# The shared expert's down product made while combining, two experts' first weights loaded while routing

## What is computed

```python
def swiglu(t, wg, wu, wd):
    return (jax.nn.silu(t @ wg) * (t @ wu)) @ wd

def moe_ffn(t, router_w, router_bias, w_gate, w_up, w_down, sh_gate, sh_up, sh_down):
    scores = jax.nn.sigmoid((t @ router_w).astype(jnp.float32))
    _, idx = lax.top_k(scores + router_bias.astype(jnp.float32), TOP_K)
    wts = ... / jnp.sum(wts, axis=-1, keepdims=True) * ROUTED_SCALE
    ...
    routed = jnp.zeros((n_tok, d), jnp.float32).at[buf_tok].add(y)   # y: swiglu of each expert's rows * weight
    shared = swiglu(t, sh_gate, sh_up, sh_down).astype(jnp.float32)
    return (routed + shared).astype(t.dtype)

x = x + gf_x * moe_ffn(h_x, *moe_args).reshape(x.shape)
return rms_norm(x, final_norm_g)
```

## Time and profile before

| what | value |
|---|---|
| median of three runs | 2757.75 us |
| the profiled execution's own time | 2765.79 us |
| its span in the trace | 2764.1 us |
| shared_and_route, first to last VectorE work | 1534.3 to 1650.1 us |
| of it, from the placed rows to the next phase | 1621.5 to 1653.8 us |
| experts | 1653.8 to 2641.4 us |
| combine | 2641.5 to 2764.1 us |
| TensorE busy over the whole span | 2502.3 us (91%) |
| DMA over the whole span | 408.11 MB, mean 148 GB/s |

### The profile page before, as it was taken

How to read it: one execution, slowest core, us unless ns; L and a number is a source line. 1 busy time by engine, 2 the same in 40 slices (tenths; PEclk the granted TensorE clock), 3 DMA queues, 4 the chain that set the end, 5 groups by cost and what they waited for, 6 DMA issues and landing times. The chain is left out here.

```text
span 2764.1 us, 72353 instructions
## 1 busy us (share of the span) xinstructions
PE 2502.3 (91%) x27195; PEld 1374.4 (50%) x27196; DVE 1542.4 (56%) x2685; ACT 973.6 (35%) x1707; POOL 840.7 (30%) x654
## 2 busy tenths in 40 slices
PE   5999899889799699899889788899999999999956
PEld 2448358735599545799644343333333333333322
DVE  3106365843578603566634676566666666666538
ACT  2613115512222112333111104455555555555411
POOL 1000000000255100111000004566666666666565
PEclk9999998989999899999889998999999999999978
DMA  6001402120000110000122127999998899672187
GB/s 254 9 0 47 140 16 92 49 63 16 1 4 4 28 48 1 3 5 4 64 100 92 58 79 315 347 353 350 367 353 317 322 343 346 260 273 83 69 320 311
DMA packets 109099, 408.11 MB, mean 148 GB/s; under 512 B 21001, under 2 KB 37083, under 8 KB 83932
## 3 DMA queue, kind: packets, MB, share of 16 engines
q1 hardware_dynamic: 76636, 287.71, 28.5%
q0 software_dynamic: 20736, 75.51, 7.0%
q10 hardware_dynamic: 11520, 41.95, 3.7%
HBM read 346.40 MB, written 58.72 MB: 147 GB/s over the span
## 5 line engine op out<-in xcount | busy, mean ns | idle before, releaser
L3271 PE MATMUL bank<-arena 128*32 x1280 | 570.0, 599 | 9.0 <-ACT arena L3338 5.9
L3273 PE MATMUL bank<-arena 128*32 128x512 f32 x3840 | 571.1, 599 | 0.0
L3232 POOL COPY arena<-arena 128x2048 f32 x240 | 450.4, 1910 | 331.3 <-PE bank L3305 314.3
L3271 PEld LDWEIGHTS bank<-arena 128*32 128x32 f32 x1280 | 135.1, 110 | 358.9 <-issue 349.9
L3302 PE MATMUL bank<-arena 128*32 x640 | 290.6, 597 | 5.5 <-POOL arena L3232 5.5
L3305 PE MATMUL bank<-arena 128*32 128x512 f32 x1920 | 291.7, 597 | 0.0
L3426 DVE COPY arena<-arena 128x2048 f32 x80 | 138.4, 1731 | 205.5 <-PE bank L3273 181.4
L3363 ACT COPY arena<-arena 128x2048 f32 x80 | 152.0, 1900 | 200.4 <-PE bank L3273 133.5
L3222 POOL DMA_INDIRECT arena<-normed_rows,arena x80 | 163.8, 2048 | 149.5 <-DVE arena L3410 137.5
L1262 PE MATMUL bank<-arena 64*64 64x64 f32 x4480 | 165.3, 220 | 13.6 <-DVE arena L1334 5.4
L3302 PEld LDWEIGHTS bank<-arena 128*32 128x32 f32 x640 | 70.5, 110 | 198.7 <-issue 198.2
(11 more groups left out here) (555 smaller groups left out, 4652.3 us busy)
## 6 DMA issues: line engine op xcount, KB each, us to landing
arena<-in_exp_w_gate_dram SPq DMA_DIRECT2D x64, 1024.0 KB
arena<-in_exp_w_up_dram SPq DMA_DIRECT2D x64, 1024.0 KB
arena<-in_exp_w_down_dram SPq DMA_DIRECT2D x64, 1024.0 KB
expert_rows<-arena ACTq DMA_DIRECT2D x80, 512.0 KB
arena<-in_w_mod_dram SPq DMA_DIRECT2D x32, 512.0 KB, 10.9
arena<-in_x_dram SPq DMA_DIRECT2D x16, 512.0 KB, 8.5
arena<-in_w_mod_dram SPq DMA_DIRECT2D x8, 1024.0 KB, 17.6
arena<-in_w_in_dram SPq DMA_DIRECT2D x12, 384.0 KB
```

Of the source, the lines that this page charges most:

```text
L3232: last = nc.gpsimd.tensor_copy(down_copy(u), down_of(slots[u]))
L3271: nc.tensor.matmul(out(SUB - 1), XTT[:, b.q, c, rows(SUB - 1)], W[:, :, c], start=first, stop=end)
L3273: last = nc.tensor.matmul(out(u), XTT[:, b.q, c, rows(u)], WC[:, u, :, c], start=first, stop=end)
```

## The change

The shared down product leaves shared_and_route. Its hidden rows `HID` are stored to a new DRAM tensor `hid_dram` (two stores of 512 KB), and `X1` is stored right at the start of the phase, as it is. In combine TensorE makes the product of a tile at the head of the tile's group in the same two banks, before the five gathered rows are added (four products of 128x512 per tile). The gate multiply and the add into `X1` that combine has anyway then cover both.

What combine reads (`X1` 4 MB, `HID` and the shared down weights 1 MB each) is loaded in the experts' phase, once the last experts' slots are free, into the slots of experts 59 to 62. `ACC` and `OUT` of combine lie in the slot of expert 63.

Gate and up of experts 0 and 1 are loaded in shared_and_route. For that the ring lies at the top of SBUF, shifted by one slot, so the slot table gets one more add.

In the last block the three copies of the downs are made by VectorE, ScalarE and GpSimd, one each.

```diff
@@ shared_and_route: the loads and stores of SP
             sp.dma_start(WU, kc(wu[0])).then_inc(gu_in, 16)
-            sp.dma_start(WD, wd[0].rearrange("(p c) n -> p c n", c=2)).then_inc(d_in, 16)
+            for e in range(BEFORE):                                  # BEFORE = 2
+                gate_up_to(sp, WGU, exp_wg, exp_wu, bass.ds(e, 1), e, first)
             for t in range(XT):
-                sp.wait_ge(base, 2 * t + 2)
                 sp.dma_start(base_dram[t * P:(t + 1) * P, :], X1[:, t]).then_inc(st, 16)
+            for f in range(2):
+                sp.wait_ge(hid, 2 * f + 2)
+                sp.dma_start(hid_dram[:, f * SEQ:(f + 1) * SEQ], HID[:, f]).then_inc(hid_st, 16)
             sp.wait_ge(st, 16 * XT)
+            sp.wait_ge(hid_st, 32)
+            sp.wait_ge(first, 32 * BEFORE)
@@ TensorE
-            pe.wait_ge(d_in, 16)
-            pe.wait_ge(hid, 4)
-            for n in range(2 * XT):
...
-                for f in range(2):
-                    last = nc.tensor.matmul(ps[1 + n % 4][:, :], HID[:, f, t * P:(t + 1) * P],
-                                            WD[:, f, half * 512:(half + 1) * 512], start=(f == 0), stop=(f == 1))
-                last.then_inc(dn, 1)
@@ VectorE
-            nc.vector.tensor_reduce(bx[:, 0], nb_le[:, :, 0:NE - 1], AX.X, ALU.add).then_inc(bex_t, 1)
+            chain(nc.vector.tensor_reduce(bx[:, 0], nb_le[:, :, 0:NE - 1], AX.X, ALU.add))
+            TS(bx[:, 0], bx[:, 0], float(SLOT0), None, ALU.add).then_inc(bex_t, 1)
...
-            for n in range(2 * XT):
...
-                TT(T[:, n % 2], ps[1 + n % 4][:, :], k.gate[1][:, c], ALU.mult).then_inc(out, 1)
-                dve.wait_ge(out, n + 1)
-                TT(X1[:, n // 2, c], X1[:, n // 2, c], T[:, n % 2], ALU.add).then_inc(base, 1)
@@ experts: SP
             for e in range(RING):
-                gate_up(bass.ds(e, 1), e)
+                if e < BEFORE:
+                    sp.sem_inc(loaded[e], 32)
+                else:
+                    gate_up(bass.ds(e, 1), e)
                 down(bass.ds(e, 1), e)
...
+            for n, e in enumerate((NE - 5, NE - 4, NE - 3)):
+                copied, read = released(e)
+                if n == 2:
+                    hold(sp, hi_d, copied)
+                    hold(sp, hi_a, copied)
+                    hold(sp, up, read)
+                    sp.dma_start(HS, hid_dram).then_inc(late_in, 16)
+                    sp.dma_start(WS..., sh_down...).then_inc(late_in, 16)
+                hold(sp, dcopy, copied)
+                hold(sp, dn, read)
+                for t in (2 * n, 2 * n + 1):
+                    sp.dma_start(tiles[t], base_dram[t * P:(t + 1) * P, :]).then_inc(late_in, 16)
...                                                # tiles 6 and 7 after expert NE - 2
+            sp.wait_ge(late_in, 16 * (XT + 2))
@@ experts: the last block (GpSimd copies only piece SUB - 2 there)
+            pe.wait_ge(last_d, 1)
+            pe.wait_ge(last_a, 1)
             widen(Turn.at(NBLK - 1))
@@ ScalarE, after the last fold
+            act.wait_ge(dn, LAST_B + 1)
+            nc.scalar.copy(down_copy(1), down_of(slot)).then_inc(last_a, 1)
@@ VectorE, after the last step
+            dve.wait_ge(dn, LAST_B + 1)
+            nc.vector.tensor_copy(down_copy(0), down_of(slot)).then_inc(last_d, 1)
@@ combine: SP
-            for t in range(XT):
-                sp.dma_start(X1[:, t], base_dram[t * P:(t + 1) * P, :]).then_inc(base_in[t], 16)
@@ TensorE
             for t in range(XT):
-                pe.wait_ge(diag, t + 1)
                 if t >= 2:
                     pe.wait_ge(added, t - 1)
+                for h in range(2):
+                    for f in range(2):
+                        nc.tensor.matmul(ps[2 * (t % 2) + h][:, :], hidden[:, f, t * P:(t + 1) * P],
+                                         down[:, f, h * 512:(h + 1) * 512], start=(f == 0), stop=False)
+                pe.wait_ge(diag, t + 1)
                 for i in range(BY_PE):
...
-                                                start=(i == 0), stop=(i == BY_PE - 1))
+                                                start=False, stop=(i == BY_PE - 1))
```

More of the change, by code:

```diff
@@ L32, with gate_slot, gate_up_to @@
 DRING = 5
+BEFORE, SLOT0 = 2, 1
+GATES_AT = 52800 - RING * 2 * KC * ED
+def gate_slot(e):
+    return (e + SLOT0) % RING
+def gate_up_to(sp, WGU, wg, wu, e, r, done):
+    for n, w in enumerate((wg, wu)):
+        sp.dma_start(WGU[:, gate_slot(r), n], w[0, e].rearrange("e (p c) n -> p (e c) n", c=KC)).then_inc(done, 16)
 BIG = 1e30
@@ L2856, in shared_and_route @@
     TOK_F, COUNT, ID2 = cr.take(XT), cr.take(P), cr.take(NE)
-    LT = cr.take(2, 512)
+    LT = HID[:, 0].rearrange("p (a n) -> p a n", a=2)
     BF, RF = cr.take(XT, TOPK), cr.take(XT, TOPK)
@@ L2860, in shared_and_route @@
     OH_R, OH_B = cr.take(HOT, TOPK, P), cr.take(HOT, TOPK, NBLK)
+    first = sem("first_experts_loaded")
+    assert cr.at <= GATES_AT + SLOT0 * 2 * KC * ED, ("shared", cr.at)
+    WGU = Carve(cr.arena, GATES_AT).take(RING, 2, KC, ED)
     flat = lambda b: b.rearrange("p t e -> p (t e)")
@@ L3119, in experts @@
     ID = cr.take(2, 1).bitcast(I32)
+    WD = cr.take(DRING, 2, D)
+    assert cr.at <= GATES_AT, ("exp", cr.at)
+    WGU = Carve(cr.arena, GATES_AT).take(RING, 2, KC, ED)
     ps = k.ps
+    gates_of = lambda e: WGU[:, gate_slot(e)].rearrange("p g c n -> p (g c n)")
+    downs_of = lambda e: WD[:, e % DRING].rearrange("p f n -> p (f n)")
+    late_in = sem("combining_loaded")
+    tiles = [downs_of(e)[:, h * D:(h + 1) * D] for e in (NE - 5, NE - 4, NE - 3) for h in range(2)]
+    tiles += [gates_of(NE - 2)[:, h * D:(h + 1) * D] for h in range(2)]
+    HS, WS = gates_of(NE - 3)[:, 0:2 * SEQ], gates_of(NE - 3)[:, 2 * SEQ:2 * SEQ + 2 * D]
     TRIPS = NBLK // 2 - 1
@@ L3226, in copy_down @@
             def copy_down(b, n=1):
-                slots = [down_slot_of(pool, b, u) for u in range(SUB - 1)]
+                pieces = (SUB - 2,) if isinstance(b.n, int) and b.n == LAST_B else range(SUB - 1)
+                slots = {u: down_slot_of(pool, b, u) for u in pieces}
                 hold(pool, down_arrived, count_of(pool, b, SUB - 2))
@@ L3464, in _, with combine @@
                 step(*(Turn.at(n + d) if n + d < NBLK else None for d in (0, 1, 2, 3, 5)))
+            slot = down_slot_of(dve, Turn.at(LAST_B), 0)
+            hold(dve, down_arrived, count_of(dve, Turn.at(LAST_B), 0))
+            dve.wait_ge(dn, LAST_B + 1)
+            nc.vector.tensor_copy(down_copy(0), down_of(slot)).then_inc(last_d, 1)
             store(Turn.at(NBLK - 1))
-def combine(nc, k, ctx, cr, base_dram, DST, WK, y_dram, final_g, out):
+    return others, gates_of(NE - 1), tiles, HS, WS
+def combine(nc, k, ctx, late, arena, DST, WK, y_dram, final_g, out):
+    others, slot, X1, HS, WS = late
+    cr = Carve(arena, others)
     sem = lambda n: ctx.semaphore("fin_" + n)
```

75 lines of the change are left out of this document (41 added, 34 removed).

## The result

The changed kernel takes 2732.76 us (median of four runs, 2731.20 to 2733.68), the kernel before 2758.36 (2757.09 to 2759.70) beside it: 25.6 us less, ratio 0.9893, 95% interval 0.9870 to 0.9916. Forecast were 40.5 us less and 2717.3; the range ended at 2709 and 2725. In a later batch it was 2729.80 against 2756.78, 27.0 us less (0.9899, 0.9876 to 0.9922). So the kernel got faster by some 26 us, and some 14 us of the forecast are missing.

What follows compares the result with a forecast made beforehand. No single engine was taken to bound the whole span, so each phase was read for itself. Gains of 31.1 + 3.5 + 2.2 + 3.7 = 40.5 us from the median 2757.75 gave 2717.3 us, range 2709 to 2725.

Steps and rivals of the forecast that it cites:

- Routing: Routing phase: without the shared down product the experts begin at 1622.71 instead of 1653.82, a gain of 31.1 us.
- rival C: Routing: the shared gate and up weights land late among 10.8 MB, 13.5 us lost, 2730.8 us; chance 5%.
- Experts, start: Experts' first blocks: earlier second turn, no wait at block 1 and a better TensorE clock gain 3.5 us (1.2 to 5).
- block 1's wait: Experts' start: TensorE's 1.32 us wait, taken as for the third gate and up, would be gone.
- blocks 4 to 7: Experts' phase: the 10.67 us of lateness there stays, since the ring of three is full; gain taken as 0.
- rival B: More than forecast: blocks 4 to 7 lose their lateness (2706.6 us), or combining's tile 0 ends earlier (2713); chance 14%.
- Last block: Experts' last block: three copies shared by three engines bring the last widen earlier, 2.2 us gained (1.0 to 4).
- Combining: Combining: TensorE becomes the bound at 12.0 us per tile; 11.4 us gained at the front, 7.7 given back, net 3.7.
- Rival A: Combining: TensorE's added 3.46 us per tile eat all that the freed DMA time brings, 2721.0 us; chance 14%.
- Rival D: Combining: TensorE stays at its lower clock, 1.2 GHz, a tile takes 24 us, slower than before at 2809 us; chance 2%.
- Late loads: Experts' phase: 6 MB loaded on SP after experts 59 to 62 are done, at cost 0.
- Rival E: Late loads of 6.3 MB happen only in front of the combining, 15 us lost, 2732 us; chance 3%.

Runs made afterwards that it cites:

- the second trace of before: The kernel before the change, unchanged, profiled a second time: 2754.64 us, one run.
- the run with held loads: Changed kernel, but SyncE holds its 7 MB of loads until the gathers of blocks 0 and 1 have landed: 2729.23 us, ratio 0.9880.
- the reads ahead: Changed kernel with the last block's slot and count table reads ahead of the waits: 2726.38 us, ratio 0.9863; timed again 2726.92, 0.9875.
- both repairs: Changed kernel with SyncE's loads held until two gathers landed, and the last block's table reads ahead of their waits: 2721.91 us, ratio 0.9854.

## Why the prediction missed

**Routing, right.** Forecast 31.1 us; the traces of the changed kernel give 31.0, 31.4 and 31.3. The 14 new transfers lost nothing: L2915 starts in time, and rival C (those products late by 13.5 us) is dead. The Trainium skill ("DMA: Bandwidth & Descriptors", Queues, rings and completion order) left a late completion possible; here the operands ahead in the queue arrived on time.

**Experts, start: the step that failed first.** The first turn stayed at 10 us, as I said. The 3.5 us behind it were 1.2 for the second turn, 1.3 for block 1's wait and 1.0 for the clock; the change was +1.4 instead. The second turn did come earlier, 3.8 us after the first instead of 4.8 and 4.4. The step that failed is the wait: I wrote that block 1's wait of 1.32 us "was for the third gate and up" and put it down as gone. It was for no landing. In the kernel before, SyncE announces the third expert 28.8 us into the phase; in the changed kernel it does so at 15.1, 14.9 and 15.0, and TensorE still idles 0.98, 1.39 and 1.40 us at the same place. What stands there is its sequencer's work for the next pass: a read of the slot and one of the count from the table, then five waits that find their semaphores done. These are the read of the count, the five waits and SyncE's three announcements, before and then in the changed kernel, as duration in ns (min/median/max), first and last start:

```profile
L3133 PEldq TENSOR_LOAD <-arena x1: 301/301/301, 1682.2 to 1682.2; - x1
L68 PEldq EVENT_SEMAPHORE  x5: 51/51/51, 1682.8 to 1683.4; - x5
L3196 SPq EVENT_SEMAPHORE  x3: 17/17/17, 1662.3 to 1682.6; - x3
```

```profile
L3149 PEldq TENSOR_LOAD <-arena x1: 306/306/306, 1651.1 to 1651.1; - x1
L83 PEldq EVENT_SEMAPHORE  x5: 51/51/51, 1651.8 to 1652.3; - x5
L3213 SPq EVENT_SEMAPHORE  x3: 17/17/17, 1627.4 to 1638.6; - x3
```

Each wait took 0.05 us in both kernels, so none of them waited. In the second trace of before TensorE had passed the wait for the experts' count (1677.4) before the third announcement came (1677.6). The clock's 1.0 was no gain to count on either: block 1's passes ran slow in one of two traces before and in one of three after, at about 2 us each time.

What the forecast did not have is ScalarE's store issue, 2.3 to 3.1 us longer where SyncE, two experts ahead, issues a load just before it. It explains the loss. Measured from the phase's start, up to block 1's SiLU the changed kernel gained 0.1 to 0.5 us, traces of the same clock compared (38.66 to 38.58; 36.59 to 36.07 and 36.20). At block 2's it was 1.6 to 1.8 behind (50.43 to 52.01; 48.37 to 50.13 and 50.12). From there to block 8 both took 80.5 us in the mean. What a lead of 4 MB could still give is lost in the ring of three, which I had seen for blocks 4 to 7 and not carried to the start. The changed kernel's busy rows show it:

```profile
1643.52:1663.52 20.00, 16.17 (x126) 5.13 (x122) 14.30 (x14) 9.28 (x11) 8.52 (x4) 0.83 0.57 221
1663.52:1683.52 20.00, 18.52 (x172) 6.99 (x168) 11.40 (x19) 9.38 (x16) 13.51 (x7) 1.00 0.51 185
1683.52:1703.52 20.00, 20.00 (x184) 7.35 (x176) 13.57 (x17) 11.13 (x13) 11.46 (x7) 1.00 0.69 243
```

The DMA engines idle 31 to 49% of the time from 20 us on, since no slot is free, and the load of expert 5 goes out 67.2, 65.3 and 65.3 us in, at 65.7 and 63.7 before. Blocks 4 to 7 stayed late as forecast, 45.5, 46.5 and 44.2 us from SiLU to SiLU after 45.98 and 44.4; the part of rival B that lay there is dead. What limited the very start was the gather beside 7 MB of weights, which the run with held loads shows: SiLU of block 8 at 125.8 us against 131.3 in the mean, 5.5 us, more than the whole term (4.7 at the first turn; ScalarE's issue is short again there as well).

**Last block: the second.** Forecast 2.2 us, measured a loss of 1.0. The durations of the copies were right (ScalarE's 1.90, VectorE's 1.63). The step from the fold's end through "the copy takes 1.90" straight to "widen at 2628.1" left out what an engine does between two busy instructions: ScalarE sat 1.47 us between the fold's end (2596.10) and the copy at 2597.57, and TensorE started 1.87 us after the copy's end (2599.47). Those are reads of the tables that give the slot and the count, placed behind waits (on TensorE two, of 0.30 us each, with the work around them): moved ahead of them both are gone, and the rival (instruction fetching after the loop) with them. The changed kernel's row says so in its releaser: "issue", a wait for nothing that the timeline knows. It is the same cost that I had taken for a landing in block 1. With the reads ahead, the step came out as forecast, 3.18 for 3.3.

**Combining: right in kind, mis-sized.** TensorE is the bound at 12.02 us per tile (forecast 12.0), waits nowhere after tile 0, and its clock stays at 1.00 from then on. Of 3.7 us forecast, 2.4 came. The mis-sized term is tile 0: I put its sums at 2661.5 + 0.3, 19.6 us after the first gather, and they came after 20.2, 20.5 and 20.7. The rest is the trace that I forecast from: its second counterpart has tile 7 at 106.7, not 107.4. Rival A (nothing given back) would have been 107.4 for tile 7, the traces show 104.4 to 104.8. Rival D (the lower clock throughout) is dead with the clock at 1.00. The Trainium skill's figure for the HBM side, about 358 GB/s ("DMA: Bandwidth & Descriptors", Where 436 GB/s comes from), gives an estimate of 13.2 us from tile to tile. The traces do not agree: the tiles stood at 12.02, with 410 GB/s in the busy row above.

**Late loads, right.** SyncE issues them from 2443.56 to 2478.6, 134 us before the first gather, and the blocks keep 11.77 us. Rival E (late loads in front of the combining) is dead.

```profile
2443.56 5.66 SPq L3246 DMA_DIRECT2D arena<-rows_before_experts  x4
...
2477.76 0.80 SPq L3252 DMA_DIRECT2D arena<-rows_before_experts  x2
```

Two rivals' numbers lie near the measured 2732.76, C's 2730.8 and E's 2732, and both by accident: neither of their losses took place. Rival D's 2809 doesn't follow from its own 96 us, which give 2813.

In sum: 5.7 us were expected of the experts' phase and it became 2.5 longer, 8.2 us missing; 1.3 are missing in the combining. What is left to the 14 is 0.3 at the end and what executions differ by in unchanged phases, which I can't assign further. Of the four gains only the routing's was exact; it rested on a stretch with a single chain.

## What to carry to other kernels

A releaser named beside a gap is what came last, and not always what the gap was for: 1.32 us stood beside a landing, and with the landing 14 us earlier 0.98 to 1.40 remained. Look at the waits themselves (here 0.05 us each) before paying a term with one. A step that waits and then computes its address costs that reading behind the wait, 1.5 to 1.9 us here on ScalarE and TensorE, so put register reads ahead of the wait. A preload only counts where its successor has a place to go: with the ring full, 4 MB of lead became idle DMA, while holding back the same queue for two small gathers brought some 5 us by the traces and the medians.

## What the runs showed beside this

Issuing one DMA from ScalarE took 0.34 us in steady work, 2.1 to 2.2 us for the first one of the phase, and 4.3 to 5.1 when SyncE had begun to issue one within 2 us before (eight traces). No run separates the two parts.

In some executions three engines lay idle together in the combining while TensorE's records show no gap. This is the changed kernel's timeline:

```profile
2643.43 1.45 PE L3577 MATMUL bank<-arena 128*128 128x512 f32 x3
...
2651.07 1.57 ACT L3588 ACTIVATE arena<-arena 128x128 f32<-128x128 f32 x5 [13.10 <-DMA arena<-in_w_in_dram]
2651.14 1.29 DVE L3619 TENSOR_TENSOR arena<-arena,bank 128x512 f32<-128x512 f32 x2 [10.92 <-DMA arena<-in_w_in_dram]
...
2651.30 0.94 POOL L3550 DMA_INDIRECT arena<-expert_rows,arena  x1 [2.81 <-DMA arena<-in_w_in_dram]
```

Tile 1's last product ends about 2644.7, VectorE takes its sums 6.4 us later, and the releaser named is a load of another phase. VectorE then works 10.80 us per tile without a wait and is level again by tile 7, whose sums wait for TensorE as in the other traces, so it cost nothing. Other traces have it (with both repairs the sums of tile 1 come at 38.2 us too), others don't, and of the same kernel with the reads first one has it and one has not. Its cause stays open.

The clock after the last block's gap was the other surprise: with the same gap of 3.18 us it held at full speed in one trace, fell after some passes in two, and was low from the first in one.
